# Modulation panels 12 to 18 moved into the feed-forward products, masking bars written ahead, zero stores at a later release

## The reference

```python
def adaln(cvec, w, b):
    return jnp.split(jax.nn.silu(cvec) @ w + b, 6, axis=-1)      # shift, scale, gate, twice

def sublayer(x, shift, scale, gate, g_pre, g_post, fn):
    h = rmsnorm(x, g_pre) * (1 + scale[:, None]) + shift[:, None]
    out, aux = fn(h)
    return x + gate[:, None] * rmsnorm(out, g_post), aux

def swiglu(x, w1, w3, w2):
    return (jax.nn.silu(x @ w1) * (x @ w3)) @ w2
```

## Time and profile before

| | us |
|---|---|
| median of 3 runs | 1445.4 (1442.62 to 1448.0) |
| the profiled execution | 1442.48 |
| its span on the trace | 1440.9 |
| TensorE busy | 1349.9 (94%) |
| VectorE, ScalarE, GpSimd busy | 870.9, 738.9, 98.8 |

### The profile page before, as it was taken

The page is one execution under the profiler, slowest core; times in us unless marked ns, Lnnn a source line. Parts: engine busy times, 40 slices in busy tenths (PEclk is TensorE's granted clock), DMA queues, the critical chain, the costliest instruction groups (busy, mean ns, idle before and its releaser), DMA issues.

```text
span 1440.9 us, 18579 instructions
## 1 busy us (share of the span) xinstructions
PE 1349.9 (94%) x7178; PEld 1060.7 (74%) x7178; DVE 870.9 (60%) x1168; ACT 738.9 (51%) x961; POOL 98.8 (7%) x170
## 2 busy tenths in 40 slices
PE   7999789899999998999989899999999998899996
PEld 3997347799998877987557776667877734688884
DVE  2534676533334436789675795456966603979796
ACT  3532466622223326596264576445865403768674
POOL 0402420000000000200000200001000000000001
PEclk9999899999999999999999999999999999999998
DMA  9933997633343323323862698658997799999993
GB/s 352 306 137 120 362 372 278 212 117 117 125 149 135 108 97 117 122 83 117 295 246 107 264 400 302 231 209 298 401 324 283 264 399 409 410 384 407 377 375 132
DMA packets 132235, 358.17 MB, mean 249 GB/s; under 512 B 6236, under 2 KB 30200, under 8 KB 132024
## 3 DMA queue, kind: packets, MB, share of 16 engines
q1 hardware_dynamic: 120440, 321.53, 60.9%
q0 software_dynamic: 9344, 32.26, 6.5%
q10 hardware_dynamic: 2368, 3.23, 0.6%
HBM read 335.35 MB, written 22.55 MB: 248 GB/s over the span
## 4 chain that ended last, share of the span: by engine, by line
PE 76%; DVE 10%; DMA 5%; ACT 4%; issue 2%; POOL 2%; SPq 1%; POOLq 0%; DVEq 0%; ACTq 0%
PE bank L2313 30%; PE bank L1964 12%; PE bank L1719 7%; PE bank L1975 6%; PE bank L2261 6%; PE bank L1769 4%; PE bank L1716 3%; DMA ring<-in_moe_w_dram 2%; DMA arena<-shear 1%; DMA ring<-in_mod_w_dram 1%; DVE arena L2767 1%; DVE ring_parts L2468 1%; PE bank L2201 1%; DVE ring_parts L3007 1%; POOL arena L866 1%
## 5 line engine op out<-in xcount | busy, mean ns | idle before, releaser
L2313 PE MATMUL bank<-arena_parts 128*128 128x512 f32 x1072 | 263.3, 392 | 4.7 <-ACT arena_parts L1463 2.6
L3007 DVE TENSOR_TENSOR ring_parts<-ring,arena_parts 128x2048 fp32r<-128x2048 f32 x85 | 192.4, 2286 | 79.5 <-PE bank L2261 43.9
L2313 PEld LDWEIGHTS bank<-arena_parts 128*128 128x128 f32 x1072 | 199.3, 188 | 54.5 <-issue 11.6
L1463 ACT ACTIVATE arena_parts<-ring 128x2048 fp32r<-128x2048 f32 x85 | 161.6, 1917 | 29.7 <-DMA ring<-in_moe_w_dram 24.0
L2313 PE MATMUL bank<-ring_parts,arena_parts 128*128 128x512 f32 x504 | 135.2, 390 | 2.9 <-DVE ring_parts L3007 2.9
L1964 PE MATMUL bank<-ht_parts,arena_parts 128*128 128x384 f32 x352 | 118.3, 336 | 0.9 <-DVE xn_parts L2479 0.8
L1964 PE MATMUL bank<-ht_parts,ring_parts 128*128 128x384 f32 x352 | 117.6, 334 | 0.0
L1964 PE MATMUL bank<-xn_parts,arena_parts 128*128 128x384 f32 x352 | 117.6, 334 | 0.0
L2313 PEld LDWEIGHTS bank<-ring_parts,arena_parts 128*128 128x128 f32 x504 | 94.4, 188 | 23.8 <-DVE ring_parts L3007 4.2
L2702 DVE TENSOR_TENSOR arena<-arena,bank 128x384 f32<-128x384 f32 x22 | 12.2, 554 | 123.6 <-PE bank L1964 123.6
L1719 PE MATMUL bank<-ht_parts,ring_parts 128*128 128x384 f32 x256 | 85.7, 335 | 0.0
(11 more groups left out here) (501 smaller groups left out, 2635.6 us busy)
## 6 DMA issues: line engine op xcount, KB each, us to landing
ring<-in_moe_w_dram SPq DMA_DIRECT2D x144, 1024.0 KB, 7.1
ring<-in_mod_w_dram SPq DMA_DIRECT2D x24, 2048.0 KB, 12.4
arena<-in_moe_w_dram SPq DMA_DIRECT2D x48, 1024.0 KB, 7.0
ring<-in_ff_w_dram SPq DMA_DIRECT2D x23, 1024.0 KB, 7.8
ring<-in_w_in_odd_dram SPq DMA_DIRECT2D x6, 2048.0 KB, 8.5
ring<-in_w_in_even_dram SPq DMA_DIRECT2D x5, 2048.0 KB, 10.8
ring<-in_ff_w_dram SPq DMA_DIRECT2D x5, 2048.0 KB, 7.8
routed<-cst POOLq DMA_DIRECT2D x1, 7168.0 KB, 23.4
```

Source lines behind the costliest of these rows:

```text
L1463: act.activation(whi_moe[high_at(w, n_)], e_half(j, h), ACT.Copy).then_inc(whi_ready, 1)
L2313: ins = pe.matmul(bank[base + b][:, :], lhs[:, c_, :], rhs[:, k, 512 * b:512 * b + 512], start=(first and h == 0 and k == 0 and n_ == 0), ...
L3007: dve.tensor_tensor(e_half(j, h, low=True), e_half(j, h), whi_moe[high_at(w, 2 * j + h)], ALU.subtract).then_inc(wlo_ready, 1)
```

## The change

It does six things.

- Modulation panels 12 to 15 are a group of their own (`G_DENSE`), multiplied after f = 3, 5, 7 and 9 of the up products; panels 16 to 18 another (`G_DOWN`), after f = 5, 8 and 12 of the down products. Attention keeps panels 4 to 11, started at units 0, 3, 6, 9, 12, 14, 16, 18; its group is turned at unit 22 and not after the last. The recurrence keeps five panels, 19 to 23.
- The order of the panels and their slots follow (`slots_`): up panels alternate between slots 1 and 0, modulation panels there have slot 2; from the odd input on slots go 0, 1, 2 in turn. SP waits for the panel that was in the slot before (`before_in_slot`). `E_SLOT` is as it was.
- The first down panel is split before the last f of the up products, and TensorE doesn't wait for the last product any more before it begins the down products.
- GpSimd fills the sheared table in DRAM with -1e30 and writes the 16 columns in the window over it, in 21 small DMAs; the masking steps are gone. VectorE waits for the gathers themselves.
- The stores of zeros wait for `up_done` 4, not for `ot_dve` 4.
- High halves are numbered by up and down panel, not by place in the ring.

```diff
         def panel_slot(i):
-            return (2, 0, 2, 0)[i] if i < 4 else i % RING
+            return slots_[i]
+        def before_in_slot(i):
+            return max(j for j in range(i) if panel_slot(j) == panel_slot(i))
...
-        panels += [mod_panel(m) for m in range(4, 16)]
+        panels += [mod_panel(m) for m in range(4, 12)]
...
+        for j in range(KF // 2):
+            panels.append((("up", j), [("lo256", cut(I["ff_w1"][0], 256 * j, 256)),
+                                       ("hi256", cut(I["ff_w3"][0], 256 * j, 256))]))
+            m = 12 if j == 1 else 10 + j
+            if j == 1 or 3 <= j < 6:
+                panels.append(mod_panel(m))
+        for j in range((KF + 3) // 4):
+            if j == 3:
+                panels += [mod_panel(16), mod_panel(17)]
+            panels.append((("down", j), [("rows", rows_cut(I["ff_w2"][0], 4 * j, min(4, KF - 4 * j)))]))
+            if j == 3:
+                panels.append(mod_panel(18))
...
-        panels += [mod_panel(m) for m in range(16, 23)]
+        panels += [mod_panel(m) for m in range(19, 23)]
         last_panels = [(("out1", j), [("k512", cut(I["w_out_odd"][0], 512 * j, 512))]) for j in range(2)]
         panels += [last_panels[0], mod_panel(23), last_panels[1]]
+        slots_ = [2, 0, 2, 0] + [1, 2, 0] * 4 + [1, 2] + [0, 2]
+        slots_ += [2 if key[0] == "mod" else 1 - key[1] % 2 for key, _ in panels[20:35]]
+        slots_ += [2, 0, 1, 2, 2, 0, 2, 1, 2]
+        slots_ += [(0, 1, 2)[n % 3] for n in range(len(panels) - 44)]
...
             for i in range(5, NP0):
-                sp_.wait_ge(*released(i - RING))
+                sp_.wait_ge(*released(before_in_slot(i)))
                 load(i)
...
-            return 4 + i // 2 if i % 2 == 0 and i < 24 else None
+            return {0: 4, 3: 5, 6: 6, 9: 7, 12: 8, 14: 9, 16: 10, 18: 11}.get(i)
...
+            barred = pts[:, 3, 0:256]
+            pool.memset(barred, NEG).then_inc(zeroed, 1)
+            pool.wait_ge(zeroed, 5)
+            pool.dma_start(shear.rearrange("h c r k -> (h c r k)").rearrange("(p n c) -> p n c", p=P, c=256),
+                          barred.unsqueeze(1).to_broadcast([P, 7, 256])).then_inc(bias_in, 16)
+            pool.wait_ge(bias_in, 16)
+            for c0_, n_, step, at_, at_step in ((0, 8, -1, 0, 0), (8, 49, 0, 0, 1), (57, 7, -1, 48, 0)):
...
-            pool.wait_ge(ot_dve, 4)
+            pool.wait_ge(up_done, 4)
             for dst in (routed[:, :], answered[OVER_AT - 2 * P:N_SLOTS, :]):
...
+                if f == KF - 1:
+                    split_down(0)
                 act.wait_ge(gate_done, f + 1)
...
-            split_down(0)
             split_down(1)
...
+                if f in (3, 5, 7, 9):
+                    mod_mm(12 + (f - 3) // 2)
+                if f == 12:
+                    mod_turn(G_DENSE)
             pe.wait_ge(gb_kept, 4)
-            pe.wait_ge(prod_ready, KF)
...
+                if f == 5:
+                    pe.wait_ge(silu_ready, KF)
+                if f in (5, 8, 12):
+                    mod_mm({5: 16, 8: 17, 12: 18}[f])
+                if f == 16:
+                    pe.wait_ge(prod_ready, KF)
+                    mod_turn(G_DOWN)
...
-            mod_mm(16)
+            mod_mm(19)
...
-                mod_mm(16 + u)
+                if u in (2, 4, 6, 7):
+                    mod_mm({2: 20, 4: 21, 6: 22, 7: 23}[u])
```

More of the change, by code:

```diff
@@ L389, in low_half, with high_half @@
             return ring_r[:, panel_slot(i), HALF * h:HALF * h + HALF]
+        def high_half(i, h, whi):
+            what, j = panels[i][0]
+            return whi[(2 * (j if what == "up" else j + KF // 2) + h) % WHI]
         def parts_of(i, h, whi, k):
-            return (whi[(2 * i + h) % WHI].rearrange("p (k n) -> p k n", k=k),
+            return (high_half(i, h, whi).rearrange("p (k n) -> p k n", k=k),
                     low_half(i, h).rearrange("p (k n) -> p k n", k=k))
@@ L605, in mod_bank @@
         def mod_bank(m):
-            return (7, 5, 2, 2)[m] if m < 4 else 7 if m < 16 else 3
+            return (7, 5, 2, 2)[m] if m < 4 else 7 if m < 12 else 6 if 16 <= m < 19 else 3
         def turn_bank(m):
             return (4, 4, 3, 3)[m]
-        MOD_GROUPS = [(m, m + 1) for m in range(4)] + [(4, 16), (16, 22), (22, 24)]
-        G_ATTENTION, G_MEMORY, G_LAST = 4, 5, 6
+        MOD_GROUPS = [(m, m + 1) for m in range(4)] + [(4, 12), (12, 16), (16, 19), (19, 22), (22, 24)]
+        G_ATTENTION, G_DENSE, G_DOWN, G_MEMORY, G_LAST = 4, 5, 6, 7, 8
         def group_of(m):
@@ L819, in _ @@
             pool.dma_start(vb[:, 3, :], I["cache_b_v"][0, 0].rearrange("s h e -> s (h e)")).then_inc(even_in, 16)
-            for k_ in range(7):
-                pool.dma_start(shear[:, :, k_, :],
-                              bass.AP(tensor=I["b_rpb"].tensor, offset=(k_ + 4) * 31 + 15,
-                                      ap=[[465, B_HEADS], [-1, GRID_W], [1, GRID_W]])).then_inc(bias_in, 16)
-            pool.wait_ge(bias_in, 16 * 7)
+            barred = pts[:, 3, 0:256]
[5 more added lines that the diff above has]
+            for c0_, n_, step, at_, at_step in ((0, 8, -1, 0, 0), (8, 49, 0, 0, 1), (57, 7, -1, 48, 0)):
+                row = 7 * GRID_W
+                for k_ in range(7):
+                    pool.dma_start(bass.AP(tensor=shear.tensor, offset=c0_ * row + k_ * GRID_W + at_,
+                                           ap=[[GRID_W * row, B_HEADS], [row + at_step, n_], [1, 16]]),
+                                  bass.AP(tensor=I["b_rpb"].tensor, offset=(k_ + 4) * 31 + 15 + at_ - (c0_ if not at_step else 8),
+                                          ap=[[465, B_HEADS], [step, n_], [1, 16]])).then_inc(bias_in, 16)
+            pool.wait_ge(bias_in, 16 * 22)
             pool.dma_start(wg[:, :, :], cut(I["w_in_odd"][0], 2048, 16)).then_inc(odd_in, 16)
@@ L857, in _ @@
                         shear[:, :, k_:k_ + 4, :].rearrange("h c r k -> c h r k")).then_inc(bias_in, 16)
-            pool.wait_ge(bias_in, 16 * (7 + 4))
-            for half in range(2):
-                v = bias[64 * half:64 * half + 64, :, :, 0:256].rearrange("p q h (r c) -> p (q h) r c", r=4)
-                lo = v[:, :, :, 0:48]
-                hi = v[:, :, :, 16:64]
-                for qh in range(16):
-                    then(pool.affine_select(out=lo[:, qh], in_=lo[:, qh], compare_op=ALU.is_ge, fill=NEG,
-                                            base=8, pattern=[[0, 4], [1, 48]], channel_multiplier=-1))
-                    ins = pool.affine_select(out=hi[:, qh], in_=hi[:, qh], compare_op=ALU.is_gt, fill=NEG,
-                                             base=8 - 16, pattern=[[0, 4], [-1, 48]], channel_multiplier=1)
-                    if qh < 15 or half == 0:
-                        then(ins)
-            ins.then_inc(zeroed, 1)
-            pool.wait_ge(zeroed, 6)
             pool.wait_ge(roped, 8)
@@ L1271, in _ @@
                     keep_gate(1, 1)
+                if f == 11:
+                    keep_mod(G_DENSE)
                 if f >= KF - F_RING:
                     hidden_hi(f - KF + F_RING)
-            split_down(0)
             split_down(1)
@@ L1283, in _ @@
                     act.activation(sp[:, 1, :], sp[:, 0, :], ACT.Exp, scale=-1.0).then_inc(soft_exp, 1)
+                if f == 14:
+                    keep_mod(G_DOWN)
             act.wait_ge(fl_ready, KF)
@@ L2674, in _ @@
                     scale_head_even(i - 21)
-            add_group(G_ATTENTION)
+                if i == 23:
+                    add_group(G_ATTENTION)
             low_head(0, 0)
@@ L2702, in _ @@
                 dve.tensor_tensor(actt[:, f, :], silt[:, f % 2, :], bank[7][:, 0:T], ALU.mult).then_inc(prod_ready, 1)
+                if f == 13:
+                    add_group(G_DENSE)
                 if f >= KF - F_RING:
@@ L2737, in _ @@
                     decay_rates()
+                if f == 16:
+                    add_group(G_DOWN)
                 if f == 5:
```

23 lines of the change are left out of this document (10 added, 13 removed).

## The result

| | us |
|---|---|
| kernel before, five runs | 1447.15 median (1442.62 to 1448.2) |
| changed kernel, five runs | 1483.68 median (1482.68 to 1485.81) |
| ratio | 1.0262, 95% interval 1.0245 to 1.028 |
| profiled execution of the changed kernel | 1483.33, its span 1481.6 |

The changed kernel is 2.6% slower. The forecast was 1491.1, within 1464 to 1503. Profile against profile the loss is 40.85 us, where the sum gave 45.7.

What follows compares the result with a forecast made beforehand. TensorE was taken to carry 76% of the chain of waits, with DMA short in attention. Terms -16 + 8.4 + 28.3 - 4 + 6.5 - 1 + 23.5 = +45.7 gave 1488.2 profiled, 1491.1 us median, range 1464 to 1503.

Steps and rivals of the forecast that it cites:

- Attention, -16: Attention: four fewer modulation products and no masking steps end it about 16 us earlier, bounds 12 and 19.
- the walk of 2.4 us a unit: Attention: VectorE sets the pace at 2.4 us a unit, so unit 16 begins at 176.5 instead of 190.95.
- The bound of 12: Attention: gain of only 12 us if panels and not VectorE set the pace to the end.
- First product, +8.4 and a gap of -4: First feed-forward product: four modulation products and a turn add 8.4 us; splitting the first down panel earlier saves 4 after it.
- The stall, +28.3: First feed-forward product: zeros delay modulation panel 13; TensorE stands 26.2 us, then runs on the low clock; bounds 0 and 30.
- One packet for one: DMA engines beside the zeros: GpSimd's and SP's queues alternate packet by packet, whatever the size.
- Rival (a): DMA queues: sharing by time or bytes, or many SP packets a turn; stall 0 to 9, 1463 to 1472 us; 13%.
- An idle under 10 us in the first case makes (a) right: Sign in the trace: TensorE's idle at the sixth f's modulation product, forecast some 26 us; under 10 favours Rival (a).
- rival (b): Panels, not VectorE, pace attention, and two-slot rings stall a little in the feed-forward products; 1499 to 1505 us; 8%.
- Second product, +6.5: Second feed-forward product: three modulation products and a turn add 6.5 us, bounds 5 and 10.
- Recurrence, -1: Recurrence: three products fewer save 1 us, since they fill TensorE's waits; bounds 0 and -5.
- The late expert load, +23.5: Behind the output product: expert's first load comes late, ScalarE's split delays the norm 21.9, cold TensorE adds 1.6; bounds 20, 26.

Runs made afterwards that it cites:

- masks_again: Changed kernel with zeros released by the head turns and two ring slots exchanged, plus GpSimd's masking steps back and no bars; 1458.11 us, ratio 1.0095.
- zeros_at_f3: Changed kernel with the stores of zeros released one f earlier, at up_done 3 instead of 4; 1486.29 us, ratio 1.028.
- zeros_at_heads: Changed kernel with the stores of zeros released by the last head turns again (ot_dve 4); 1467.8 us, ratio 1.0144.
- slot_and_rec: Changed kernel with zeros at the head turns, panel 23 in the expert's slot, and modulation panels 16 to 18 back in the recurrence; 1436.86 us, ratio 0.9945.
- expert_slot: Changed kernel with two slots exchanged, so modulation panel 23 takes the slot of the expert's first panel; 1465.22 us, ratio 1.0137.
- bars_alone: Kernel before with only the bars written into the DRAM table ahead and no masking steps on GpSimd; 1443.83 us, ratio 0.9994.

## Why the prediction was right, point by point

**The sign and the two causes** were right: a late modulation panel under the zeros, and a late expert load in front of the norm. Each was taken away by one line, and each gave back what the stage table says. The mechanism was right in both; that the total came within 7.4 us of 1491.1 is in part luck, since the stall was 11.5 us too large in the sum and most other terms were too small.

**Attention, -16.** It gave -13.9 in its stage. Unit 16 began at 178.56 on VectorE, 36.5 us after the stage's first modulation product; the walk of 2.4 us a unit gave 35.8. Panel of unit 9: product at 162.98 behind an idle of 1.41, forecast 161.7 and under 1. What failed is the last term: from unit 16 to the out-projection it is 34.71 us, and 34.77 before. The turn and the waits that I took off there, 1.9 us, were not on the path. The bound of 12 had room for that. The small transfers cost nothing, as forecast: GpSimd's idle time ahead of the cosine products is 34.52 us, and it was 51.15.

**Input, 0.** TensorE reached attention 1.4 us later. The changed kernel and the ten experiments reach it at 141.5 to 143.2, masks_again too, which has no bars; so it is probably the profiled execution of before, at 140.69, that was early. It also lay 4.7 us under the median of its five runs. So part of the 40.85 us between the profiles is probably that one execution; the medians differ by 36.5. No second profile of before is there to show it.

**First product, +8.4 and a gap of -4.** Without the zeros the stage is 5.1 us longer than before (195.84 against 190.75), the sum gave 4.4. Right.

**The stall, +28.3.** Measured +16.8, the 21.9 of the stage less the 5.1 above: two waits of 7.1 us, and two products of 3.48 and 3.41 for 1.92. The mechanism and its place were right; this is the term of the sum that was mis-sized, by two steps. The first is that up panel 3 "lets 130 of the zeros' 176 pass", one for one from its issue on: the zeros' queue came to the engines 5.9 us after its issue, when 1899 of up panel 3's 2080 packets had gone alone. The second is the price of a pair, taken as the sum of two single packets: 0.178 + 0.052 = 0.230 us. The pair takes 16 x 4 / 337 = 0.190 us of an engine (338 beside 336 in 4 us), and one with a 2 KB packet 16 / 68 = 0.235, where the sum of singles is 0.267.

An estimate of the two shares: with the pairs' own prices my sum would have been 130 x 0.190 + 46 x 0.235 + 18 x 0.089 = 37.1, with a start and a landing 38.1, so a wait of 19.6 and some 21.7 us in all. The price of the pair was thus some 6.6 of the 11.5, the head start some 4.9. zeros_at_f3, where the queues do meet, bears it out: 18.2 us at panel 13, and a stage of 215.99 us, 20.3 longer than in zeros_at_heads.

Because of the head start, the sentence "Up panel 4 follows panel 13 and lands 8 us later" was wrong as well: of the 176 packets an engine some 110 were still to come when panel 13's 64 were through, up panel 4 alternated with them, and panel 14 behind it was late by 7.1. Stores that have not met the first panel meet the third.

**One packet for one.** Right, also for 1 KB beside 4 KB. Rival (a) had the queues share by time or by bytes, or SP get many packets a turn. It is out by the earlier trace rows and by the changed kernel's own rows, though by equal time it gave a stall of 7 to 9 at panel 13, which the first wait of 7.1 happens to match. So my sign, "An idle under 10 us in the first case makes (a) right", was a bad one: the idle is under 10, and what decides is the packets, 338 beside 336, and the second wait, which (a) did not have. Its time, 1463 to 1472, lies below the measured one too. Of rival (b), stalls of the two-slot ring without the zeros, nothing is seen: in zeros_at_heads no matmul of either feed-forward product waits for a DMA. The Trainium skill, "DMA: Bandwidth & Descriptors", section "Queues, rings and completion order", has an engine drain some 9 to 17 descriptors of one ring before it switches. If the trace's packets of 1, 2 and 4 KB are such descriptors, the rows don't agree with it: 338 to 336, 68 to 68.

**Second product, +6.5.** Measured +5.9 (98.87 against 93.02). But the stage of before had 1.5 us of slow matmuls in it from the gap: slot_and_rec, with neither, has 91.56. So the three products and the turn cost 7.3, of which 6.3 are their own time, and the gap's removal gave back about 5 where I had 4. Two small errors of opposite sign.

**Recurrence, -1.** Measured +0.8, and the twelve kernels lie between 188.1 and 190.8, with no order by the number of products (188.5 to 190.8 with eight, 188.1 to 190.8 with five). It is 0 as far as the scatter lets one see: the three products had been free where they were.

**The late expert load, +23.5.** Measured +23.7, and 23.7 back in expert_slot. The order of steps in three programs and the durations of the earlier trace rows gave the steps to the tenth: the squares began 10.5 us behind the output product's end, forecast 10.6, and the last root was done 26.1 behind it, forecast 26.2. TensorE's slow start took the rest.

**Sum.** Terms measured from attention's start: -13.9 + 0.9 + 21.9 + 5.9 + 0.8 + 23.7, with 1.4 of the input 40.7; forecast 45.7. The errors, measured less forecast: stall -11.5, attention +2.1, input and out-projection +2.3, recurrence +1.8, the rest under 1.

## What to carry to other kernels

Before a product is moved, ask whether it was free where it stood: three modulation products cost 7 us in a stage that TensorE fills and none in one whose chain runs through VectorE. When panels are renumbered, print the new slot of every panel up to the first one of the next stage; a slot that falls to the last user delays a load, and it is paid in full if two engines have the split of that load ahead of work they could do. A bulk store takes the DMA engines for its own time wherever it runs; put it where no panel with a due time is issued. Here that is behind the head turns: from 189 to 251 us SP issued nothing in the changed kernel. The stores just fit: in zeros_at_heads they were issued at 217.45 and their last packet stands at 251.3, 0.8 us before SP's next load.

## What was not expected of the hardware

A queue that comes second to busy engines starts late, whichever it is. GpSimd's stores reached the engines 2.2 us after their issue on empty engines, and 4.6 to 5.9 us after it while SP's queue was sending 1 and 2 KB packets. SP's up panels reached them 1.0 us after their issue on empty engines, and 3.8 to 4.6 us after it while GpSimd's queue was sending 4 KB ones. These few microseconds decided which panel was late. The Trainium skill, "DMA: Bandwidth & Descriptors", section "Latency and other measured facts", gives about 1 us until the first byte of a DMA on GpSimd's queue; small ones in the kernel before come near it (issued at 985.37 and 579.82, first packets 1.1 and 1.4 us later), the 7 MB store on empty engines took the 2.2.

Idle time costs TensorE more than its length. Behind 3.60 us of idle, eight matmuls took 1.6 us more; behind the waits of 7.1 us a modulation product took 3.4 to 3.5 us for 1.9; behind 8.4 us in bars_alone, 3.56. The granted clock goes with it. In the changed kernel's windows it is 0.54 over the product behind the first wait and 1.00 over the matmuls that follow it:

```profile
323.80:327.30 3.50, 3.44 (x17) 0.63 (x17) 0.00 (x0) 0.00 (x0) 0.00 (x0) 0.54 1.03 411
327.40:331.00 3.60, 3.60 (x21) 3.60 (x22) 0.00 (x0) 0.00 (x0) 0.00 (x0) 1.00 1.04 414
```
